# Attention on TensorE: turns and values in batches of three groups instead of two, values three groups behind

## What is computed

```python
def attend_block(args):
    s_c = jnp.einsum('bqgjd,bngd->bqgjn', q_blk, k_cmp).astype(f32) - slopes[:, :, None] * dist_c[None, :, None, None, :].astype(f32)
    p_c = masked_softmax(s_c, (dist_c >= 0)[None, :, None, None, :])
    o_c = jnp.einsum('bqgjn,bngd->bqgjd', p_c, v_cmp)
    imp = jnp.einsum('bqgjn,nm->bqgm', p_c, cover)
    ...
    _, top = lax.top_k(imp, top_k)
    ...
    p_s = masked_softmax(s_s, (dist_s >= 0)[:, :, :, None], axis=(-2, -1))
    o_s = jnp.einsum('bqgjkl,bqgkld->bqgjd', p_s, v_g.astype(f32))
    ...
    p_w = masked_softmax(s_w, valid_w[None, :, None, None, :])
    o_w = jnp.einsum('bqgjs,bsgd->bqgjd', p_w, v_blk.astype(f32))
    o = g_blk[:, :, 0, :, :, None] * o_c + g_blk[:, :, 1, :, :, None] * o_s + g_blk[:, :, 2, :, :, None] * o_w
```

## Time and profile before

| | |
|---|---|
| median of 3 runs | 3088.87 us (3087.88 to 3094.94) |
| profiled execution, its own time | 3087.6 us |
| its span | 3085.9 us |
| TensorE busy | 2914.6 us, 94% |
| attention, from the first turn to the last value | 1698.7 to 2253.4 us |
| mean granted clock of TensorE | 0.979 |

### The profile page before, as it was taken

One profiled execution on the slowest core, in us unless ns is written; L12 is line 12 of the kernel. 1 busy time (PEld: TensorE's weight loads), 2 busy tenths in 40 slices (PEclk: granted clock), 3 DMA queues, 4 the chain that ended last, 5 costly groups with the idle time before them and its releaser, 6 DMA issues. The chain is left out here.

```text
span 3085.9 us, 43401 instructions
## 1 busy us (share of the span) xinstructions
PE 2914.6 (94%) x17327; PEld 2343.1 (76%) x17327; DVE 1226.9 (40%) x2021; ACT 954.9 (31%) x1626; POOL 1407.6 (46%) x920
## 2 busy tenths in 40 slices
PE   6998999989999999999995888889999999999998
PEld 4887878877888888888784666555687888888887
DVE  5455463524331331332202677745514331331334
ACT  3444441322330110121101555777713320210211
POOL 2444434656444444444630555545536444444442
PEclk9998999989999999999997999999999999999999
DMA  4100011021111111111114000000011111111111
GB/s 141 47 23 2 15 35 48 15 89 41 48 50 52 48 45 50 48 45 53 42 34 126 2 1 1 1 1 1 15 35 42 48 48 49 51 46 52 48 44 72
DMA packets 212558, 127.57 MB, mean 41 GB/s; under 512 B 9016, under 2 KB 208189, under 8 KB 212285
## 3 DMA queue, kind: packets, MB, share of 16 engines
q1 hardware_dynamic: 210797, 125.32, 13.8%
q10 hardware_dynamic: 1616, 0.21, 0.0%
HBM read 112.94 MB, written 8.39 MB: 39 GB/s over the span
## 5 line engine op out<-in xcount | busy, mean ns | idle before, releaser
L486 POOL TENSOR_TENSOR WH<-WR,ONES 128x1024 fp32r<-128x1024 f32 (+1 forms) x192 | 452.2, 2355 | 1138.4 <-PE PS L1847 964.1
L1847 PE MATMUL PS<-YH,WH 128*128 128x512 f32 x1904 | 590.0, 391 | 5.3 <-POOL WL L489 4.1
L1847 PE MATMUL PS<-YH,WL 128*128 128x512 f32 x1904 | 587.2, 390 | 0.0
L1847 PE MATMUL PS<-YL,WH 128*128 128x512 f32 x1904 | 587.2, 390 | 0.0
L489 POOL TENSOR_TENSOR WL<-WR,WH 128x1024 fp32r<-128x1024 f32 (+1 forms) x192 | 456.0, 2375 | 15.1
L1612 DVE SCALAR_TENSOR_TENSOR X<-PS,PTF,X 128x1023 f32<-128x1023 f32 (+1 forms) x176 | 225.7, 1282 | 562.3 <-ACT X L1090 549.5
L1847 PEld LDWEIGHTS PS<-YH,WH 128*128 128x128 f32 x1904 | 357.3, 188 | 82.3 <-POOL WL L489 4.5
L1847 PEld LDWEIGHTS PS<-YH,WL 128*128 128x128 f32 x1904 | 357.9, 188 | 74.8
L1847 PEld LDWEIGHTS PS<-YL,WH 128*128 128x128 f32 x1904 | 358.0, 188 | 74.6
L1090 ACT ACTIVATE X<-PS,PTF 128x1024 f32<-128x1024 f32 x88 | 106.2, 1207 | 830.3 <-PE PS L1847 823.8
L716 POOL TENSOR_SCALAR X<-X,STAT,SM 128x640 f32<-128x640 f32 (+6 forms) x215 | 176.5, 831 | 163.8 <-DVE STAT L1767 163.7
(11 more groups left out here) (404 smaller groups left out, 3942.7 us busy)
## 6 DMA issues: line engine op xcount, KB each, us to landing
WR<-in_ffn_w_up_dram SPq DMA_DIRECT2D x88, 512.0 KB, 3.8
WR<-in_hy_w_in_dram SPq DMA_DIRECT2D x28, 512.0 KB, 3.8
WR<-in_ffn_w_down_dram SPq DMA_DIRECT2D x32, 448.0 KB, 3.5
WR<-in_ffn_w_down_dram SPq DMA_DIRECT2D x16, 512.0 KB, 3.7
WR<-in_nsa_w_in_dram SPq DMA_DIRECT2D x14, 512.0 KB, 3.7
X<-in_x_dram SPq DMA_DIRECT2D x8, 512.0 KB, 7.2
xt_scratch<-H SPq DMA_DIRECT2D x1, 4096.0 KB, 13.3
WR<-in_hy_w_out_dram SPq DMA_DIRECT2D x8, 512.0 KB, 3.7
```

The costliest lines, as they stand in the source:

```text
L486: pool.tensor_tensor(WH[:, slot, 0:k, :], WR[:, slot, 0:k, :], ONES[:, :].unsqueeze(1).broadcast_to([P, k, P]), ALU.mult).then_inc(w_hi, 1)
L1847: ins = pe.matmul(PS[:, 2 * slot + a, :], w[:, slot, i, :], y[:, i, a * HALF:(a + 1) * HALF], start=(i == 0 and w is WH and y is hi), stop ...
```

## The change

Two of three numbers. TensorE takes three groups in a batch, and values lie three groups behind the turns; VectorE's output steps move back by one group with `LAG`. Turn banks (two), PTR buffers (five), score banks and `AHEAD` stay.

```diff
-        BATCH, LAG, AHEAD = 2, 2, 3
+        BATCH, LAG, AHEAD = 3, 3, 3
```

## The result

| | before | with the change |
|---|---|---|
| median | 3089.18 us (4 runs) | 3200.73 us (4 runs, 3194.35 to 3202.26) |
| ratio, 95% interval | | 1.0354 (1.034 to 1.0369) |
| span of the profiled execution | 3085.9 us | 3200.5 us |
| attention, first turn to last value | 554.7 us | 664.1 us |

What follows compares the result with a forecast made beforehand. TensorE's own work and its waits were taken to set the attention stage's length. Terms -17 + 47 + 15 + 43 - 16 = +72 us, on 3087.6 plus 1.3 to the median, gave 3161 us, range 3105 to 3215.

Steps and rivals of the forecast that it cites:

- the upper end: Top of the predicted range, 3215 us; the forecast's own bounds, with upper-end waits and no relief, reached 3223.
- The clock rival: TensorE in attention: short waits lower the granted clock from 0.97 to 0.90, +39 us, so 3200; chance 0.15.
- Switches, -17: TensorE in attention: 56 fewer batches, each saving 0.31 us of switching between turns and values, -17 us.
- Third turns, +47 and +15: TensorE in attention: third turns wait for ScalarE to copy out their bank, +47 us; late copies add +15.
- Two scores in a batch, +43: TensorE in attention: 31 second scores instead of 2 wait for VectorE's bias of the first, +43 us.
- Given back, -16: Attention: batches with one score hide VectorE's bias better; half of TensorE's 33.0 us wait before scores goes, -16 us.
- Sum: All terms together: +72 us in the attention stage, giving 3161 us for the kernel.
- the signs named beforehand: Profile after: turns' copy waits over 110 cases, 85 us or more; fewer, longer score waits; "issue" about 112; stage near 627 us.
- trade places: Attention: new waits only replace waits for VectorE and GpSimd that would have come anyway, +4 us, 3093; chance 0.08.
- faster: Attention: switches are the true cost, copies are hidden, third turns wait under 0.1 us; -29 us, 3060; chance 0.07.
- The local check on the stall-free stretch: Timeline of 2082 to 2099 us: 15 groups taking 18.1 us would lose 3.1, scaled to 336 groups 69 us.

Runs made afterwards that it cites:

- batches of one: The kernel before with one group per batch instead of two, values still two groups behind: 3105.4 us, ratio 1.0049.
- 46 by the run: The change, but in batches with several steps' scores only the first stand before the turns, the others behind them: 3154.7 us, ratio 1.0217.
- output steps late: The change, with VectorE's output steps five groups behind in its list instead of three, TensorE's list unchanged: 3145.7 us, ratio 1.0178.
- output steps four back: The kernel before (batches of two, values two behind), VectorE's output steps four groups back instead of two: 3099.0 us, ratio 1.0034.
- threes: Batches of three: the change (3200.7 us) against the same with values two groups behind, VectorE's output steps left three back (3164.4 us, ratio 1.0245).
- twos: Batches of two: the kernel before against the same with values three groups behind instead of two (3103.7 us, ratio 1.0043).
- output steps three back: The kernel before (batches of two, values two behind), VectorE's output steps three groups back instead of two: 3079.6 us, ratio 0.9964.
- all three remedies: The change with second scores behind the turns, third turn behind the first values, and VectorE's output steps five groups back: 3122.0 us, ratio 1.0098.

## Why the prediction was right, and where not

The direction, the two new waits and the range were right; the forecast was 40 us short, because it let the first scores' wait fall when it rose, and left the clock out. That the range held all the same owes something to luck: these two faults were partly covered by a term that was too high, and the upper end had been put together from the worst cases of other terms. The clock rival's 3200 us is the measured time by chance: it needed a clock of 0.90, and the stage had 0.95. Step by step:

- **Switches, -17.** The price of 0.31 per batch stands, seen by itself in batches of one. (The rows that I took it from, give 0.14 behind turns, and 0.17 behind 12 values but 0.22 behind 16, where scores follow.)
- **Third turns, +47 and +15.** The wait is there, and of the size I gave it: third turns' weight loads wait 59.2 us for copies, in 99 cases. In the change's timeline (below) the third turn starts 2153.05 - 2151.71 = 1.34 us after the first where I had 1.27. I had read two copies in 1.08 us as 0.54 each; they overlap, and a single one takes 0.59 (median of all 336). In the stage's balance the term shows as only 39 (69.5 - 30.7), since the other turns, which had waited 30.7 us for copies, now wait 10.3: 23 less than my 62.

```profile
2151.71 1.09 PE L2522 MATMUL PS<-IDENT,X 128*128 128x128 f32 x8
2153.05 0.66 PE L2522 MATMUL PS<-IDENT,X 128*128 128x128 f32 x4 [0.25 <-ACT Z L1142]
```

- **Two scores in a batch, +43.** 49 by the waits (51.8 - 2.8), 46 by the run. Right.
- **Given back, -16.** This step failed, with the sentence "TensorE never waits for it there" on VectorE's output step. It is true that nothing waits for the output step itself. What waits is the bias queued behind it. I had named that for batches with a pair and still let it take only half of a relief. First scores wait 52.7 us, 22 more than the 31.0 of before, instead of 16 less: a miss of 38. With output steps late they wait 4.1. The row that told it was among, VectorE's 64.7 us for values: a wait in an engine's list is not free if what stands behind it is on the path.
- **The clock, a rival at 0.15.** The stage's clock was 0.95, not 0.97. The time lost at half speed is (1 - 0.95) x 664.1 = 33 us where it was (1 - 0.97) x 554.7 = 17: +17, as an estimate, and the forecast had it at zero. That is under half of the rival's 39. TensorE's busy time grew by the same 17.0, but that agreement is partly chance, as busy time also holds the switches saved and a part of each third turn's wait (in the rows above the turn starts 0.46 us later than eight turns need, and 0.25 shows as idle). The Trainium skill, TensorE: Matmul & The Clock Gate, section "A second HAM failure mode: psum-queue depth-cycling", says of another kernel that short idles between groups make the clock swing. The trace agrees here, with 17 us. The run with output steps four back does not: less idle than before, and a clock of 0.94.
- **Sum.** The stage grew by 109 us where 72 was forecast. The steps above give 38 + 17 + 6 - 23 = 38, and turns wait 5 us less for GpSimd's scaling (10.7 instead of 15.5): 33 of the missing 37.

Of the signs named beforehand, the third turns' waits came in 110 cases but with 69.5 us, not 85, "issue" in 93 cases, not 112, and the stage took 664 us, not 627. Scores were to wait in fewer but longer cases; they waited in more, 70 instead of 42, which is the failed step again.

The rivals "trade places" and "faster" fell: turns that waited for a copy left TensorE idle 35.9 / 76 = 0.47 us each, not under 0.1. The local check on the stall-free stretch gave 69 us and had the same hole, since in that stretch no bias stood behind a late output step. It was also miscounted: the 6.04 us of the earlier trace rows hold four groups, not five, and 18.1 us hold twelve, not fifteen. Redone with its own prices it is -0.62 + 1.7 + 1.75 = +2.8 us for twelve groups, 79 us in all, so its agreement with 72 was chance.

What stays open: the values' third group of delay costs 36 us in threes and 14 in twos. In threes it reaches TensorE through the first scores (52.7 us with it, 16.2 without), while turns wait for copies as long either way. Whether the PTR buffers help to make values late is not separated: ScalarE's copies waited 37.8 us in 43 cases for them in the change, and their number was not varied. With output steps late, copies still waited 31.4 us for them and first scores only 4.1, so first scores hardly hang on them there. A third bank for turns was not tried, as the stage uses all eight PSUM banks.

## What to carry to other kernels

Before a producer's batch is made longer than the number of its buffers, take the timeline of one batch: if the consumer's latency (here 1.34 us) exceeds what the producer can do before it needs the first buffer back (0.88), every batch pays the rest. In an engine that works its list in order, look at what is queued behind each wait: an add of 0.29 us that nobody waits for held back biases, and moving it two groups later in the list gave 55 us. Remedies need not add: three that gave 134 us apart gave 79 together here.

## What the runs showed that I had not expected

The granted clock took part in several results, and not in step with TensorE's idle time. Output steps four back on the kernel before left less idle (57.1 us instead of 60.7) and a lower clock (0.94 instead of 0.97), and the kernel got slower. Executions of one kernel differ by it too: the six with output steps three back go from 3074.0 us (whole-program clock 0.980) to 3088.8 (0.974). A stage read from a single profile carries this scatter, so differences of under about 10 us between two profiles are better taken from the medians.

Outside the changed stage there is a scatter of 5 us between executions: TensorE's first scores of the attention start at 1681.35 us in the profile of before and at 1686.68 in the change's. Of two other runs that share all lists up to there with it, the one with late output steps started at 1681.4 and the one with all three remedies at 1686.7. So of the 114.6 us between the two spans 109.4 are the change's.
